# A hybrid decoder step on one core: mixer preparation threaded between the projection's tiles

## The reference

```python
x = x + 0.5 * swiglu(rmsnorm(x, g1), wg1, wu1, wd1)          # D_FF 2816
h = rmsnorm(x, g_mix) @ w_in                                  # 1024 -> 3397
qa, ka, va (6 heads)  qf, kf, vf, ff (5 heads)  qc, fc, ic, gc (5 heads) = split(h)
qa, ka = rope(qa), rope(ka)
oa = moba(qa, cached + new ka, va)         # 256-key blocks, best 3 past blocks + own
of = fox(qf, kf, vf, logf=log_sigmoid(ff + b))                # forgetting attention
oc = hgrn2(silu(qc), k=(1-lb)*sigmoid(-fc), ic, log f)        # gated recurrence
oc = rmsnorm(oc) * silu(gc)
x = x + concat(oa, of, oc) @ w_out
x = x + 0.5 * swiglu(rmsnorm(x, g2), wg2, wu2, wd2)
```

## Time and profile before

| | us |
|---|---|
| three runs, median (lowest to highest) | 1786.49 (1783.93 to 1787.73) |
| the profiled execution | 1789.04 |
| its span | 1787.4 |
| PE busy in the span | 1663.8 (93%) |
| DVE busy | 1084.8 (61%) |
| ACT busy | 669.8 (37%) |
| POOL busy | 162.1 (9%) |

### The profile page before, as it was taken

One profiled execution on the slowest core, in us unless ns is written; L12 is line 12 of the kernel. 1 busy time (PEld: TensorE's weight loads), 2 busy tenths in 40 slices (PEclk: granted clock), 3 DMA queues, 4 the chain that ended last, 5 costly groups with the idle time before them and its releaser, 6 DMA issues. The chain is left out here.

```text
span 1787.4 us, 36002 instructions
## 1 busy us (share of the span) xinstructions
PE 1663.8 (93%) x13569; PEld 1537.6 (86%) x13569; DVE 1084.8 (61%) x1815; ACT 669.8 (37%) x960; POOL 162.1 (9%) x329
## 2 busy tenths in 40 slices
PE   5999999979989789999999999999798887999997
PEld 5999999966667579999999999999566666999996
DVE  7666555456577556665566665543676755766645
ACT  3333232235544424333333323322565443433332
POOL 0000000021333300000000000000224331000000
PEclk9999999989989889999999999999899997999998
DMA  6444445546666634444444444554657574444443
GB/s 191 141 154 152 139 145 141 156 135 185 216 195 214 195 125 160 146 143 151 140 154 155 150 135 153 159 141 126 188 182 243 191 217 147 160 159 141 138 151 116
DMA packets 284179, 287.46 MB, mean 161 GB/s; under 512 B 26542, under 2 KB 272998, under 8 KB 283942
## 3 DMA queue, kind: packets, MB, share of 16 engines
q1 hardware_dynamic: 268290, 239.52, 43.2%
q0 software_dynamic: 14464, 46.48, 8.2%
q10 hardware_dynamic: 1316, 0.03, 0.1%
HBM read 279.58 MB, written 6.40 MB: 160 GB/s over the span
## 5 line engine op out<-in xcount | busy, mean ns | idle before, releaser
L1505 PE MATMUL PS<-xh,whi 128*128 128x320 f32 x1920 | 596.4, 311 | 13.8 <-DMA K<-in_consts 10.2
L1505 PE MATMUL PS<-xh,wlo 128*128 128x320 f32 x1920 | 593.9, 309 | 0.0
L1505 PE MATMUL PS<-xl,whi 128*128 128x320 f32 x1920 | 593.8, 309 | 0.0
L609 ACT ACTIVATE whi<-raw 128x2048 fp32r<-128x2048 f32 (+2 forms) x185 | 340.5, 1841 | 610.0 <-PE PS L1505 602.9
L894 DVE TENSOR_TENSOR wlo<-raw,whi 128x2048 fp32r<-128x2048 f32 (+2 forms) x185 | 406.8, 2199 | 262.0 <-ACT whi L609 260.0
L1505 PEld LDWEIGHTS PS<-xh,whi 128*128 128x128 f32 x1920 | 361.0, 188 | 15.9 <-issue 10.4
L1505 PEld LDWEIGHTS PS<-xh,wlo 128*128 128x128 f32 x1920 | 361.1, 188 | 0.6
L1505 PEld LDWEIGHTS PS<-xl,whi 128*128 128x128 f32 x1920 | 361.0, 188 | 0.0
L1505 PE MATMUL PS<-hh,whi 128*128 128x320 f32 x704 | 217.5, 309 | 0.0
L1505 PE MATMUL PS<-hh,wlo 128*128 128x320 f32 x704 | 217.5, 309 | 0.0
L1505 PE MATMUL PS<-hl,whi 128*128 128x320 f32 x704 | 217.5, 309 | 0.0
(11 more groups left out here) (252 smaller groups left out, 1832.5 us busy)
## 6 DMA issues: line engine op xcount, KB each, us to landing
raw<-in_ffn_w_gate SPq DMA_DIRECT2D x45, 1024.0 KB
raw<-in_ffn_w_up SPq DMA_DIRECT2D x45, 1024.0 KB
raw<-in_ffn_w_down SPq DMA_DIRECT2D x32, 1024.0 KB
raw<-in_w_in SPq DMA_DIRECT2D x64, 512.0 KB
key_pages<-in_cache_moba_k SPq DMA_DIRECT2D x128, 192.0 KB, 2.5
value_pages<-in_cache_moba_v POOLq DMA_DIRECT2D x128, 192.0 KB, 2.9
key_pages<-in_cache_fox_k SPq DMA_DIRECT2D x128, 160.0 KB, 3.2
value_pages<-in_cache_fox_v POOLq DMA_DIRECT2D x128, 160.0 KB, 3.4
```

Source lines behind the costliest of these rows:

```text
L609: act.activation(whi[s][:, 0:nk, :], raw[s][:, 0:nk, :], ACT.Copy).then_inc(hi_done[s], 1)
L1505: last = te.matmul(out, w[wslot][r, kt, cols], x[r, at, :], start=start and n == 0 and m == 0, stop=stop and n == len(ktiles) - 1 and m == 2)
```

## The change

The doubled tile goes (31 tiles, the last chunk half wide). The tile order becomes qa, qf, ka, kf, ff, qc, fc, gc, va, vf, ic. The projection is written out tile by tile on PE, DVE and ACT, and the transition's steps are put behind chosen tiles. The token transposes now use two PSUM banks, bank 6 read by DVE for even groups and bank 7 read by ACT for odd ones, so that group m waits for the copy of group m - 2. The mask of the new keys moves from `weight_rows` (which lies over `raw`) to `b[4]`. The three ring units of the transition leave the ring of PSUM banks. The recurrence's products and scans leave the block loop.

```diff
-for _n in ("qa", "qf", "ka", "kf", "va", "vf", "ic", "ff", "qc", "fc", "gc"):
+for _n in ("qa", "qf", "ka", "kf", "ff", "qc", "fc", "gc", "va", "vf", "ic"):
...
-TILES += [TILES[-1]]
...
# SP
-                sp.wait_ge(rows_copied_dve, L * 9 + 9)
+                sp.wait_ge(forget_copied, L + 1)
+                sp.wait_ge(rows_copied_dve, L * 8 + 8)
...
# ACT
+                for c in range(2, WIN_CHUNKS):
+                    hi(c % 2, L * USES + OFF["win"] + c // 2, 8, 256 if c < WIN_CHUNKS - 1 else 128)
...
+                    if c == 10:
+                        act.wait_ge(z_ready, L * 2 + 1)
+                        act.activation(tmp[2][0:BH, :], tmp[1][0:BH, :], ACT.Exp, scale=-1.0).then_inc(z_exp, 1)
+                        copy_rows(1)
+                        copy_rows(3)
+                    if c == 11:
+                        act.wait_ge(z_ready, L * 2 + 2)
+                        act.activation(tmp[1][0:BH, :], tmp[2][0:BH, :], ACT.Ln).then_inc(z_exp, 1)
+                        copy_rows(5)
+                    if c == 12:
...
+                        act.activation(of(1), p3(T["qc"]), ACT.Sigmoid).then_inc(rec_sigmoids_ready, 1)
...
+                for m in (7, 9, 11, 13):
+                    copy_rows(m)
# DVE
+                for t in range(WIN_TILES):
+                    projected(t)
+                    if t in (9, 11, 13):
+                        rope(t - 9)
+                    if t == 17:
+                        copy_rows(0)
+                    if t == 25:
+                        rec_queries()
+                    if t == 27:
+                        rec_gates()
+                    if t % 2 == 1 and t // 2 + 2 < WIN_CHUNKS:
+                        c = t // 2 + 2
+                        lo(c % 2, L * USES + OFF["win"] + c // 2, 8, 256 if c < WIN_CHUNKS - 1 else 128)
...
+                    if t in (9, 11, 13):
+                        rope(t - 8)
+                    if t == 15:
+                        forget_logits()
+                    if t == 17:
+                        forget_exps()
+                    if t == 18:
+                        copy_rows(2)
+                    if t == 19:
+                        forget_logs()
+                        copy_rows(4)
+                    if t == 20:
+                        new_mask()
+                    if t == 21:
+                        decode_queries()
+                    if t == 22:
+                        copy_forget()
+                    if t == 23:
+                        new_forget()
...
+                    if t == 25:
+                        mask_new_scores()
+                    if t == 27:
+                        link(dve.memset(key_pages[:, :, AW + BW:], 0.0))
+                        give(pads_cleared)
+                        copy_new_scores()
+                        copy_rows(6)
+                    if t == 28:
+                        copy_rows(8)
+                    if t == 29:
+                        rec_keys(0)
+                        copy_rows(10)
+                give(win_used)
+                rec_keys(1)
...
+                copy_rows(12)
+                copy_keys(0, 1)
+                copy_rows(14)
+                rec_keys(2)
# PE
+                def turn_rows(m):
...
+                    if m >= 2:
+                        te.wait_ge(rows_copied_act if m % 2 else rows_copied_dve, L * (7 if m % 2 else 8) + m // 2)
...
+                for t in range(WIN_TILES):
...
+                    if t in (9, 11, 13):
+                        rotate(t - 9)
+                        rotate(t - 8)
+                    if t in (16, 17, 18):
+                        turn_rows(2 * t - 32)
+                        turn_rows(2 * t - 31)
+                    if t == 21:
+                        turn_forget()
+                    if t == 23:
+                        new_scores()
+                    if t == 26:
+                        turn_new_scores()
+                        turn_rows(6)
+                        turn_rows(7)
+                    if t == 27:
+                        turn_rows(8)
+                    if t == 28:
+                        turn_rows(9)
+                        turn_rows(10)
+                turn_rows(11)
+                te.wait_ge(win_used, L * 32 + 36)
...
+                turn_rows(12)
+                turn_rows(13)
                 for u in range(3):
                     turn_keys(0, u)
+                turn_rows(14)
```

More of the change, by code:

```diff
@@ L168, in ring_units @@
     for L in range(DEPTH):
-        order += [(L, "forget"), (L, "new", 0), (L, "new", 1)]
         order += [(L, "keys", 0, u) for u in range(3)]
-        order += [(L, "new_turned")]
         for i in range(BLOCKS):
@@ L1591, in _, with rotate @@
                 ffn(0, L)
[L1593 to L1613 removed]
+                def rotate(n):
+                    te.wait_ge(win_used, L * 32 + 4 + ROPED[n] + 1)
                     if n >= 2:
@@ new lines, in new_scores @@
+                def new_scores():
+                    te.wait_ge(decode_queries_ready, L + 1)
+                    te.wait_ge(forget_copied, L + 1)
+                    settle(te)
+                    new_keys = lambda pr: pt(T["ka"] + pr)[:, SEQ:NT]
+                    for g in range(4):
+                        last = te.matmul(PS[0:NS, 4, 128 * g:128 * g + 128], new_keys(g + 1), qz[:, :, 2 * g, 0:16], start=True, stop=True)
+                    last.then_inc(new_scores_ready, 1)
+                    te.matmul(PS[0:NS, 5, 0:128], new_keys(0), qz[:, :, 1:4:2, 16:24], start=True, stop=True)
+                    te.matmul(PS[0:NS, 5, 128:192], new_keys(5)[0:64], qz[0:64, :, 5, 16:24], start=True, stop=True).then_inc(new_scores_ready, 1)
```

342 lines of the change are left out of this document (164 added, 178 removed).

## The result

| | before | after |
|---|---|---|
| median of four runs (lowest to highest), us | 1785.63 (1783.93 to 1787.73) | 1822.66 (1819.75 to 1825.47) |
| ratio, 95% interval | | 1.0210 (1.0193 to 1.0227) |
| span of the profiled execution, us | 1787.4 | 1823.8 |
| PE busy in the span, us | 1663.8 | 1668.9 |
| mean granted clock in the span | 0.959 | 0.944 |

The forecast was 1798, within 1776 to 1812. The sign was right; of 37 us the working had 11.8.

A forecast was written before the change was run, and what follows sets the result against it. The projection was taken as bound by PE alone, the transition by handshakes. Per layer -3.5 + 23.8 - 16.4 + 3 - 1 = +5.9, twice +11.8, giving 1798 us against the median of 1786.49; range 1776 to 1812.

The forecast's parts named there:

- The doubled tile: Projection: leaving out one tile per layer saves 3.5 us, all on the path.
- What is added to the projection: Projection: work and waits moved between its tiles cost 23.8 us per layer, 13.9 of it waits.
- Rival 1: Projection: waits do not form because copies come before PE asks; 1764.5 us; chance 0.15.
- The clock: Projection: PE's pauses lower its clock for the work behind them; 3 us per layer, bounds 0 and 6.
- The block loop: Blocks 2 to 7: 6 us of DVE work leave, gaining 1 us per layer, bounds 0 and 3.
- The transition: Last tile to the third block's key turning: shrinks from 34.4 to 18 us, 16.4 gained per layer.
- I add 1 us: Transition: 1 us allowed for value pages colliding with states and outputs on the DMA engines.
- the working's 11.7 and 16.5 to 17: Transition, us after PE's last tile matmul, without collision: page 4 issued at 11.7, its keys turned at 16.5 to 17.
- Rival 2: Transition: page 4 does not bind, 24.3 us gained per layer; about 1776.5, or 1782.5 with clock loss; chance 0.15.
- Rival 3: Projection waits hold, clock falls at each gap, DMA collision takes its upper bound; 1806 to 1812 us; chance 0.20.

The follow-up runs named there:

- the run with a shift alone: Changed kernel plus four unused matmuls behind tile 4 of each projection, so all that follows comes 2.1 us later; ratio 1.0175 to the kernel before.
- a sister kernel: Changed kernel with the projection's copies and transposes moved by a tile or less so that no transpose waits; ratio 0.9965 to the kernel before.

## Why the prediction was wrong

**The doubled tile, -3.5 per layer: right** (8 us in two layers, 5 to 11).

**What is added to the projection, +23.8: right.** 9.9 of work, measured as 9.8 and 10.1. 13.9 of waits, measured as 13.0 and 12.9 us of idle PE. Single points: group 3 at 4.4 us after PE's end of tile 17 (4.25 forecast), 5.49 ahead of tile 28 (5 to 6), no wait at the others. Rival 1 fell with it in this kernel. In the run with the copies re-placed its condition came true, since the waits were a matter of a tile's distance; its time did not: 1764.5 was worked out for it, and 0.9965 is 1780.

**The clock, +3, bounds 0 and 6: inside its bounds for the projection** (4.5 and 5.5), **and wrong in where it was counted.** The working priced only the work right behind each pause of the projection and put the clock of all later stages at no change, without a reason. PE kept busy in those pauses gave 22 us in all, where the working had 6 for them: 8.4 in the projections and 13.4 in the block loops. In the changed kernel 41.3 us of the two loops are lost at 1.2 GHz, 27.1 in the kernel before.

**The block loop, -1, bounds -3 and 0: the step that failed most.** Measured +2.4 and +7.5. DVE's work did leave, and with it 1.8 and 0.6 us of PE's idle time, about what the term said. But I had taken the loop's length apart from that as given, and it is not: it holds 16 and 11 us of time lost to the clock already before, and 22 and 20 in the changed kernel. In all these kernels it lay between 11 and 22 us per layer, with the same instructions on PE. One cause is shown: PE busy ahead of page 4 made the whole 6 us faster (1 to 11), nearly all of it in the first layer's loop, which began at the same moment. For the pauses in the projection it is not shown: the run that filled them also brought the loop 3.4 us earlier, and the run with a shift alone says that the moment may matter. How the 9.9 us of the two loops divide between the two stays open.

**The transition, -16.4: the second step that failed,** by 2.7 us at the third block's keys (20.7 instead of 18, just inside the bound of 21). The term "I add 1 us" for the collision of value pages, states and outputs was mis-sized: 3.9 us, shown by the run without the value pages, in which the working's 11.7 and 16.5 to 17 come out as 11.8 and 16.8. The ten outputs took 10.2 us to issue beside POOL's value pages and 7.5 without them. The Trainium skill (DMA: Bandwidth & Descriptors, Issuing engines are not separate DMA queues) says that DMAs of different issuers share the engines; this agrees. Measured to the end of the third block's first copy, the loss is 3.7 to 4.2.

**Rival 2, page 4 does not bind: wrong,** PE waits 13.84 us for it. But behind it stood a second bound that no rival named, the past-sum copy in POOL's queue, 1 us from the first. **Rival 3** had the right direction for both halves and was still 11 us short, since it too left the loop out.

Put together per layer: tile and projection +23.3 forecast, +24.2 and +25.5 measured; transition 4 us short; loop and rest 3 and 11 worse. That is +13.1 and +23.3 in place of +5.9 twice. In the rest of the second layer, +2.5, PE idles 2.9 us longer; no run explains that.

## What to carry to other kernels

In a list of in-order work threaded between tiles, place each copy about a whole tile ahead of the transpose that needs it: here moving four copies and three of PE's transposes by about a tile turned 2.1% slower into 0.35% faster. A pause on PE can cost more than its own length, as those of 2.67 and 5.49 us did here: look at the granted clock behind it and of the next long stretch, too, and try the price by filling the pause with unused matmuls before you redesign. Stages that nobody changed can still change by several us; run a kernel that does the same work, as the one with only a new tile order, to see by how much. When a transition is compressed, count the bytes that must now pass in it, and list what stands behind the transfers on every issuing queue.

## What the runs showed of the hardware

- 25 unused matmuls per layer in PE's pauses made a kernel 22 us faster (1.0210 to 1.0088).
- Behind a wait of 13.84 us the clock stayed at 0.50 for about 11 us of work, behind one of 14.76 us in a sister kernel for 3.6. With the second one filled by 26 matmuls it stayed at 1.00 in the first layer; in the second layer it still fell to 0.50 for some 3 us.
- The same loop, with the same 2184 or 2185 matmuls on PE, took between 185.4 and 194.5 us in the first layer of five kernels that differ only ahead of it. What decides is known in part only: what PE did just before it, and perhaps when it began.
- The fifth of ten outputs, which took 0.72 us to issue on SP's queue in the kernel before, took 2.63 with the DMA engines at a share of about 1, and held all behind it.
- Sixteen transfers issued from GpSimd occupied its queue for 16 us: a copy of 0.34 us behind them decided when TensorE could go on, in the run with the outputs spread.
